# Twelve modulation chunks of the second block's last pass: products on GpSimd in the second feed-forward stage instead of on VectorE in the block's first pass

## What is computed

```python
# the first block, per layer
mod = (cond @ w_ada[l] + b_ada[l])[:, None, :]
sh1, sc1, g1, sh2, sc2, g2 = split(mod, 6)
h = rmsnorm(x, norm1_w[l]) * (1.0 + sc1) + sh1
x = x + g1 * token_mixers(h, ...)
h = rmsnorm(x, norm2_w[l]) * (1.0 + sc2) + sh2
x = x + g2 * conv_ffn(h, w_up[l], conv_f_w[l], w_down[l])
# the second block, per pass
mod = c_silu @ w_ada + b_ada
shift, scale, gate = split(mod, 3)
z = (rms_norm(x, norm_g) * (1 + scale) + shift) @ w_in
return x + gate * (merged @ w_out)
```

## Time and profile before

| | |
|---|---|
| median of 3 runs | 2840.64 us (2836.81 to 2843.49) |
| the profiled execution | 2840.68 us |
| its span in the trace | 2838.8 us |
| mean granted clock of TensorE | 0.971 |
| TensorE busy (matmuls) | 2726.3 us, 96% |
| VectorE busy | 1797.5 us, 63% |
| ScalarE busy | 1153.7 us, 41% |
| GpSimd busy | 670.5 us, 24% |
| DMA moved | 297.37 MB, 105 GB/s |

### The profile page before, as it was taken

The page is one execution under the profiler, slowest core; times in us unless marked ns, Lnnn a source line. Parts: engine busy times, 40 slices in busy tenths (PEclk is TensorE's granted clock), DMA queues, the critical chain, the costliest instruction groups (busy, mean ns, idle before and its releaser), DMA issues.

```text
span 2838.8 us, 37346 instructions
## 1 busy us (share of the span) xinstructions
PE 2726.3 (96%) x15090; PEld 2196.1 (77%) x15090; DVE 1797.5 (63%) x2941; ACT 1153.7 (41%) x1905; POOL 670.5 (24%) x494
## 2 busy tenths in 40 slices
PE   7999899999999998999999999989999999999997
PEld 6877678888878676888887878767687788777686
DVE  5779667876567676777557768644436558545434
ACT  3233544333242454443224463344324464444322
POOL 0000046898700004256540032000110122000110
PEclk9999999999999998999999999989899999999899
DMA  7353033454432112344433435221232323221231
GB/s 239 109 167 103 29 119 126 157 177 156 141 95 67 59 58 88 106 138 147 139 114 99 151 110 156 75 64 53 75 97 78 91 67 93 79 86 53 75 97 60
DMA packets 277387, 297.37 MB, mean 105 GB/s; under 512 B 9824, under 2 KB 259808, under 8 KB 277216
## 3 DMA queue, kind: packets, MB, share of 16 engines
q1 hardware_dynamic: 264448, 247.06, 27.9%
q0 software_dynamic: 12480, 47.45, 5.0%
q10 hardware_dynamic: 288, 0.47, 0.1%
HBM read 284.73 MB, written 2.10 MB: 101 GB/s over the span
## 4 chain that ended last, share of the span: by engine, by line
PE 89%; DVE 4%; ACT 3%; issue 1%; DMA 1%; SPq 1%; DVEq 0%; ACTq 0%
PE ps L555 87%; PE ps L775 2%; DVE wl L1395 1%; DMA raw<-in_w_in 0%; ACT recat L933 0%; DVE recat L1683 0%; DMA t1s<-rawt 0%; SPq L1991 0%; ACT att_p L933 0%; DVE xT L1401 0%; DVE adaacc L1401 0%; ACT att_s L933 0%; ACT wh L933 0%; ACT s L933 0%; DVE ca L1401 0%
## 5 line engine op out<-in xcount | busy, mean ns | idle before, releaser
L555 PE MATMUL ps<-hh,wh 128*128 128x512 f32 x2208 | 895.0, 405 | 12.6 <-DVE hl L1395 4.1
L555 PE MATMUL ps<-hh,wl 128*128 128x512 f32 x2208 | 871.5, 395 | 0.0
L555 PE MATMUL ps<-hl,wh 128*128 128x512 f32 x2208 | 871.3, 395 | 0.0
L1395 DVE TENSOR_TENSOR wl<-raw,wh 128x2048 fp32r<-128x2048 f32 (+3 forms) x234 | 504.3, 2164 | 222.2 <-ACT wh L933 222.0
L555 PEld LDWEIGHTS ps<-hh,wh 128*128 128x128 f32 x2208 | 420.4, 190 | 124.5 <-issue 33.1
L555 PEld LDWEIGHTS ps<-hh,wl 128*128 128x128 f32 x2208 | 419.9, 190 | 93.7 <-issue 1.0
L555 PEld LDWEIGHTS ps<-hl,wh 128*128 128x128 f32 x2208 | 420.8, 191 | 82.4 <-issue 1.0
L933 ACT ACTIVATE wh<-raw 128x2048 fp32r<-128x2048 f32 (+3 forms) x234 | 369.9, 1591 | 170.6 <-PE ps L555 157.7
L555 PE MATMUL ps<-fh,wh 128*128 128x512 f32 x432 | 171.8, 398 | 0.0
L555 PE MATMUL ps<-fh,wl 128*128 128x512 f32 x432 | 168.4, 390 | 0.0
L555 PE MATMUL ps<-fl,wh 128*128 128x512 f32 x432 | 168.2, 389 | 0.0
(11 more groups left out here) (290 smaller groups left out, 4248.3 us busy)
## 6 DMA issues: line engine op xcount, KB each, us to landing
raw<-in_w_in SPq DMA_DIRECT2D x74, 1024.0 KB, 5.3
raw<-in_w_up SPq DMA_DIRECT2D x44, 1024.0 KB, 5.1
strewn<-in_w_ada POOLq DMA_DIRECT2D x80, 512.0 KB, 4.4
raw<-in_w_ada SPq DMA_DIRECT2D x24, 1024.0 KB, 5.3
raw<-in_w_in SPq DMA_DIRECT2D x44, 512.0 KB, 5.1
raw<-in_w_out SPq DMA_DIRECT2D x16, 1024.0 KB, 5.2
raw<-in_w_down SPq DMA_DIRECT2D x16, 1024.0 KB, 5.2
stage<-in_w_ada SPq DMA_DIRECT2D x8, 1024.0 KB, 11.4
```

Source lines behind the costliest of these rows:

```text
L555: return e.matmul(o, a, b, start=start, stop=stop, skip_group_check=True)
L1395: return e.tensor_tensor(o, a, b, op)
```

## The change

```diff
-                              (lambda: block1(1), [], 0, 0), (lambda: ffn(1), ada(1, 1, (5,)) + ada(2, 0, (1, 0, 2)), 0, 32),
-                              (lambda: block2(0), ada(2, 1, (1, 0, 2)), 3, 12), (lambda: block2(1), [], 0, 0)):
+                              (lambda: block1(1), [], 0, 0), (lambda: ffn(1), ada(1, 1, (5,)) + ada(2, 0, (1, 0, 2)) + ada(2, 1, (1, 0, 2)), 0, 32),
+                              (lambda: block2(0), [], 0, 0), (lambda: block2(1), [], 0, 0)):
```

## The result

The changed kernel takes **2857.76 us** (median of 4 runs, 2850.48 to 2861.06); the kernel before, beside it, 2838.72 us (4 runs, 2834.63 to 2843.49). The ratio is 1.0069, 95% interval 1.005 to 1.0088: slower by 0.7%. By the medians it is +19.0 us in the first set and +13.6 in the second.

A forecast was written before the change was run, and what follows sets the result against it. TensorE, 96% busy, was taken to bound the kernel. Wait +26.8, clock +2, sums +6.0 and first pass -17.5 gave +17.3 us on 2840.7: 2858 us, range 2838 to 2872.

The forecast's parts named there:

- TensorE waits for GpSimd: Second feed-forward stage: GpSimd falls behind with 28 chunks; TensorE waits, mostly ahead of the last `down` group: +26.8 us.
- low clock in the feed-forward stage: After the long wait TensorE runs a few microseconds at 1.2 GHz instead of 2.4: +2 us, bounds 0 to 4.
- sums: Twelve more chunk sums of 0.50 us on TensorE in the second feed-forward stage: +6.0 us, also leaving the first pass.
- the first pass in all: First pass of the second block, without its twelve chunks, gets shorter by four terms: -17.5 us, bounds 10.3 to 25.1.
- rival B: A wash: quick GpSimd steps, 16.7 us of wait, first pass nearly at its ceiling (-23): +1.7, 2842 us; chance 0.15.
- the end of the heads: First pass, end of the first attention: fewer head rows without a projection, so TensorE waits less: 3.4 us gained.
- The two waits for `nrm`: First pass: two TensorE waits for ScalarE's `nrm` writes, the longer 2.9 us, vanish with chunk and sum: 4.3 us gained.
- The clock term of 3.8 us: First pass: half of TensorE's 7.7 us of extra busy time at the lower clock goes: 3.8 us gained.
- the ceiling: The 25.1 us between the second block's two passes, the most that taking chunks out of the first can give.
- A: GpSimd keeps up, with a step under 12.8 us, so TensorE never waits and the kernel is faster: 2829 us; chance 0.10.
- C: GpSimd slows to 14.44 us steps, TensorE waits 39 us, VectorE's splits come late too: +31, 2872 us; chance 0.15.
- D: The products don't move, or the second pass moves too; the forecast held it excluded by the order.

The follow-up runs named there:

- e11: The changed kernel run again, unaltered, in a second set of 12 runs: 2851.62 us, ratio 1.0039 to the kernel before.
- e7: Changed kernel, but VectorE's weight split writes 2 of 2048 columns in the second feed-forward stage (output differs): 2828.71 us.
- e2: Changed kernel, but only eight of the twelve chunks move; four stay on VectorE in the first pass: 2832.44 us.
- e3: Changed kernel, but GpSimd does only the first half of each chunk in the second feed-forward stage, all sums kept: 2833.34 us.
- e10: Kernel before, with `final` as one piece ahead of the first pass's woven order; chunks stay on VectorE: 2835.81 us, ratio 0.9984.
- e5: Changed kernel, with `final` as one piece ahead of the first pass's woven order instead of four pieces within it: 2840.33 us.
- e9: Changed kernel with 26 chunks in each feed-forward stage, no flush in the second, and `final` as one piece ahead: 2817.52 us, ratio 0.9918.
- e6: As e1, with `final` also multiplying only 2 of 512 columns, its places in the order kept: 2818.76 us.
- e1: Changed kernel without the twelve chunks anywhere; the second pass's modulation is a copy of the first's: 2821.04 us.
- e4: Changed kernel without the flush of open sums ahead of the last `down` group in the second feed-forward stage: 2846.11 us.

## Why the prediction was right, and where its terms were not

The forecast was 2858 us, slower with a chance of 0.76, and the result is 2857.76. The mechanism is the one forecast, at the place forecast. That the number fits to a quarter of a microsecond is luck: the terms were off by up to 13 us, in both directions, the result's own runs spread over 10.6 us, and the second set of runs has a median 6 us lower. Forecast was +17.3 us; measured are +19.0 and +13.6 by the medians. Term by term, on the profiled executions:

| term | forecast | measured (after; e11) |
|---|---|---|
| TensorE waits for GpSimd | +26.8 | +13.8; +17.9 |
| low clock in the feed-forward stage | +2 | +5.6; +3.1 |
| sums | +6.0 | +6.0 |
| other there | 0 | +0.7; +1.2 |
| the feed-forward stage in all | +34.8 | +26.1; +28.2 |
| the first pass in all | -17.5 | -11.8; -16.7 |
| all stages whose order did not change | 0 | -4.5; -6.2 |

**The wait: right in place and cause, 1.5 to 2 times too large.** The forecast had chunk 27 ready 24 x 13.95 + 9.0 = 343.8 us after the third chunk's start. Measured are 24 x 13.68 = 328.4, and 1504.32 - 1497.64 = 6.7 for the rest: 8.7 us less. The mean of the first stage (13.95; its sum gives 13.94) was too slow for this one by 2%, which 24 steps make 6.4 us. The 9.0 us of the rest is what a chunk takes in the mean of that stage (8.8), but this one is made while TensorE stands and VectorE idles behind it, all its operations are the short ones, and it takes 6.7. That is what rival B said of a TensorE that stands, and the forecast gave it no term. The other part comes from TensorE. The forecast had it at the flush 1490.7 - 1173.66 = 317.0 us after the third chunk; it came at 1494.36, and without the 3.7 us that it had waited on the way at 1490.7, 321.4 us after 1169.24: 4.4 us later. 3.4 of them are a stretch of 6.8 us at 1.2 GHz from 1331.4 on, at the end of the wait of 2.19 us, and 0.5 the wait for VectorE. So 26.8 - 8.7 - 4.4 = 13.7, and 13.8 are there. (The sum at 1484.74 is by the trace the 15th of 16 and not the 14th; "12 more sums ahead of it" is right with that.)

What the wait lost in size went in part to the clock term: 3.4 us at that stretch and 2.2 behind the flush (half of 1504.5 to 1508.9), 5.6 where 2 was taken. In e11 the stretch at 1331 is missing, although TensorE waits 2.18 us at the same sum; there the clock costs 3.1 us (half of 6.2 us of work at the low level) and the wait is 17.9. Wait and clock together are 19.4 and 21.0 us, where 28.8 were forecast.

**The sums** hold: +6.0 us by 12 x 0.50. e7 shows them alone (383.1 - 377.2 = 5.9), e2 eight of them (3.9). e3, with the same sums, has 4.4, so a stage's length shows them to some 2 us only.

**The first pass: two of four terms held.** The sums (6.0) and the end of the heads (3.4: waits of 9.5 us became 6.1) came as they should. The two waits for `nrm` were to go with 4.3 us. The shorter went with its sum (e10, which keeps the sums, keeps it); the longer became 2.1, not 0, and 1.4 us for `rawt` came, so that 0.8 us were gained. In e11 it is 1.6 us and none for `rawt`, 2.7 gained. The step "with the chunk gone (some 4.2 us, below) it goes" failed: `final` itself and a split still stand ahead of ScalarE's copies, and this wait is gone only where `final` stands ahead (e5, e9, e10) or is cut short (e6).

The clock term of 3.8 us can be read from TensorE's busy time in the first pass, 641.94 us in before. Less the 6.0 us of sums that is 635.9; measured are 635.0 in after, so 0.9 us of clock, and 631.9 in e11, so 4.0. In the other five profiles with this end of the heads and `final` whole it is 632.3 to 636.2. The term is real in some executions and absent in others; its size was taken right, its certainty not. What failed in the reading was the ceiling: the difference of the passes, 25.1 us, could be the chunks' alone only with `final` at nothing, as the forecast said, and it then stayed with 17.5 without a term for the places of `final`. The runs divide it into some 13 for the chunks (e1) and 10 to 15 for the places that `final` has in the woven order, the index selection standing behind the last of them (e5), of which its operations themselves are some 5 (e6).

**Why each needs the other.** The heads of "a" wait for the end of the selection, and the order packs bare what comes late. That end came 280.7 us into the pass before, 277.4 with `final` ahead alone, 248.9 with the chunks gone alone, and 226.3 with both. Bare rows at the end of the heads of "a": 21, 21, 12, 2. e2, with four chunks left there, lies between: 266.5 us and 16 rows. Taking `final` to the front frees the selection's begin: its first MAX8 starts 65.2 us into the pass before, 51.5 with `final` ahead alone, 61.5 with the chunks gone alone, 45.4 with both. But while VectorE has the chunks between the selection's steps, its end comes only 3 us earlier. This is read from the orders and traces of five kernels; which cost or due time in the planner decides it was not tried.

**The rivals.** A (GpSimd keeps up, 2829) did not occur, but its mechanism is real: with the long forms mostly gone in e7 the step is 11.2 to 12.6 us and TensorE waits nowhere for GpSimd, at 2828.7 us. B (a wash, +1.7 us) is excluded by both intervals as a time; in its wait for GpSimd (16.7 us at the quick step) it was nearer than the forecast, in its first pass (-23) farther. C is out: the mean step is 13.68 and not 14.44, and TensorE waited 0.5 us for VectorE's splits. D was excluded rightly: the second pass is 638.5 us (638.7 before).

The Trainium skill (GPSIMD Engine Reference, 4.1 Engine selection) puts elementwise work on VectorE, GpSimd being about two times slower. With VectorE's split all but gone, e7, the measured step is still 11.6 us against 4.2 on VectorE, 2.8 times; with it, 3.3 times. The page's advice fits the change as it was made, not e9: that keeps all twelve chunks on GpSimd and is the quickest, because what counts is whether the slow engine's work fits under a stage that has nothing else for it.

## What to carry to other kernels

Work handed to an idle engine costs only its sums up to a pace, and the pace is set by the stage's order and not by the engine's share of the span: GpSimd was busy 29% overall, and 24 chunks in the stage cost 4 us, their sums, while 28 cost 26 to 28 us. Compare the step of the helper (here 13.7 us) with the spacing of those who wait for it (11.4), count how far it is behind at each place that drains all open work, and spread the load or move the drain (26 and 26 chunks with the flush gone: no wait, at the same step). And when a stage doesn't gain what its twin suggests, look at the order of what is left: the same edit shortened the first pass by 10 to 16 us with the chunks gone and by 3.5 at most with them there.

## What the hardware showed

- Where VectorE's instruction has two inputs in SBUF, it and GpSimd's stand in each other's way, instruction by instruction. Timeline of VectorE in after, around a split:

```profile
1173.47 1.78 DVE L1395 TENSOR_TENSOR fl<-ug,fh 128x512 fp32r<-128x512 f32 x1
...
1175.30 2.69 DVE L1395 TENSOR_TENSOR wl<-raw,wh 128x2048 fp32r<-128x2048 f32 x1
1180.66 2.98 DVE L1401 SCALAR_TENSOR_TENSOR ug<-ps,sv,ug 128x511 f32<-128x511 f32 x4 [2.68 <-ACT ug L933]
1183.56 0.79 DVE L1395 TENSOR_TENSOR fl<-ug,fh 128x512 fp32r<-128x512 f32 x1
```

Timeline of GpSimd in after, the same stretch:

```profile
1173.07 1.63 POOL L1936 TENSOR_TENSOR strewn<-strewn 128x512 f32<-128x512 f32 x1
...
1175.92 2.67 POOL L1945 TENSOR_TENSOR adaacc<-adaacc,strewn 128x256 f32<-128x256 f32 x1
...
1181.68 1.29 POOL L1936 TENSOR_TENSOR strewn<-strewn 128x512 f32<-128x512 f32 x1
```

GpSimd's addition of 1175.92 begins while the split runs (to 1177.99) and ends 0.6 us behind it, at 1178.59; alone it takes 0.72. VectorE's `fl` of 1173.47 begins beside a GpSimd addition that ends at 1174.70, and takes 1.78 us where the one of 1183.56 takes 0.79. The four operations of 1180.66, with one input in PSUM (`ps`), take their 0.75 us each beside GpSimd (in before, where GpSimd works half as much, this group has 747 ns too). In e7 no GpSimd product takes over 1.91 us (in after up to 3.40) and no 128x256 addition over 1.11. The Trainium skill (SBUF — State Buffer, SBUF: two separate sides) tells the rule: an exclusive lock on the shared ports, taken by VectorE's instructions with two SBUF inputs when GpSimd's reads SBUF; the trace agrees.
- Beside a busy GpSimd a tiny operation can be nearly all waiting. The split of e7 writes 128x2; its group of VectorE in the stage:

```profile
L1395 DVE TENSOR_TENSOR wl<-raw,wh 128x2 fp32r<-128x2 f32 x33 | 34.8, 1053 | 11.6 <-ACT wh L933 11.6
```

1053 ns in the mean; the one at 1497.14, behind GpSimd's last operation of the stage, takes 0.15 us.
- The price falls on both, and unevenly. With GpSimd's work nearly doubled in the stage (171 to 319 us busy), VectorE's 128x512 `fl` goes from 1287 to 1881 ns, its 128x2048 split from 2857 to only 3009: a short operation can lose more than its own length.
- A short stop of TensorE can cost more than itself, and need not. After the 10.1 us wait its matmuls stand at 0.63 us until 1508.9 and lose 2.2 us. The stop of 2.19 us that ends at 1331.7 went with 6.8 us at the lower level, 3.4 lost. Three other executions have the same stop of 2.18 or 2.19 us at the same sum (e11, e4, e5) and no low level there.
